# Embedding norm of a two-block transformer kernel: statistics from a second copy of x, rows normalised by VectorE alone

## The chip, the cores and the metric

The kernel runs on one core of a Trainium2 chip. The metric is the device time in microseconds (us) of one execution. TensorE (PE) multiplies matrices, VectorE (DVE) and ScalarE (ACT) work on tiles element by element, GpSimd (POOL) does so too and issues some transfers, and SyncE (SP) issues the others.

## The reference

Two blocks run one after the other on 512 tokens of width 2048. The change is in the very first step, the embedding norm `h = layernorm(x, emb_ln_g, emb_ln_b)`:

```python
def layernorm(x, g, b):
    xf = x.astype(jnp.float32)
    mu = jnp.mean(xf, axis=-1, keepdims=True)
    var = jnp.mean(jnp.square(xf - mu), axis=-1, keepdims=True)
    y = (xf - mu) * lax.rsqrt(var + LN_EPS) * g.astype(jnp.float32) + b.astype(jnp.float32)
    return y.astype(x.dtype)

def first_block(x, ...):
    h = layernorm(x, emb_ln_g, emb_ln_b)
    for l in range(DEPTH):            # DEPTH = 2
        h = hybrid_layer(h, ...)      # starts with proj = x @ w_in[l]
    return h
```

The layer rotates some columns by `cos(ang)` and `sin(ang)`, with `ang = positions * inv_freq`; these angles are the other thing the change moves.

## The kernel before, in words

All activations lie transposed in SBUF: 16 tiles `x_res` (`Y`) of 128 features by 512 tokens. A product in full precision is made of three passes of TensorE over one 128x512 tile (lines 331 to 333): `x_lo`·`w_hi`, `x_hi`·`w_lo`, `x_hi`·`w_hi`. So each activation tile is needed twice, as `x_hi` (ScalarE) and as the rest `x_lo` (VectorE, line 1109), and each weight unit of 128x1024 too: SP loads it into one of four slots, ScalarE copies it to `w_hi` (line 302), VectorE subtracts to get `w_lo` (line 325). The order on each engine is the order in which the code is written; semaphores join the engines.

**The start.** SP loads the positions, then x transposed in 16 tiles, then the first four weight units. VectorE turns the positions into angles (lines 989 to 1000), and ScalarE makes `cos_sin` from them. TensorE sums the first x tile over its features (`column_sums`), ScalarE makes of this a provisional mean `shift`, VectorE subtracts it from all 16 tiles (line 1194). Of each shifted tile ScalarE takes the squares (line 583), which TensorE adds up, and GpSimd adds the tiles themselves (line 420). `emb_end` (lines 1065 to 1074) turns the sums into a mean and a reciprocal of the deviation, both spread over all partitions. **The normalisation** then goes tile by tile: GpSimd subtracts the mean (line 390), VectorE multiplies by the reciprocal (line 1103), ScalarE writes `x_hi` and `x_res` with gain and offset (line 541), VectorE makes `x_lo` two tiles behind (line 1109).

**The first products** (`first_tiles`) work on three output tiles at once: nine passes for each of the feature tiles 0 to 7; then tiles 8 to 10 for each output tile alone, since the weight units 4 and 5 that two of them need are split only during the normalisation (`normalise(0, {13: ..., 14: ...})`); then nine passes for each of the feature tiles 11 to 15. That makes 144 passes. Output tile 3 follows with weight units 6 and 7, and in its middle (`lat_sums`, line 1881) it wants a sum from VectorE (line 1267), which stands on VectorE behind the split of unit 7. **GpSimd** waits for the last `x_lo`, issues four DMAs (lines 426, 428, 413) and scales all 16 `x_res` tiles without any wait between them (line 432).

The same normalisation is run again by two later layers (`normalise(1)`, `normalise_rms`), which keep their own way of taking statistics.

## Time and profile before

| | us |
|---|---|
| median of 3 runs | 2481.34 (2481.2 to 2482.8) |
| the profiled execution, whole | 2483.18 |
| its span in the trace | 2481.6 |
| TensorE busy | 2396.0 (97%) |
| VectorE busy | 1283.0 (52%) |
| ScalarE busy | 886.3 (36%) |
| GpSimd busy | 440.9 (18%) |

The profiled execution took 1.8 us more than the median, of which 1.6 us lie around its span. A row of a timeline gives start, duration, engine, line, what is written and read, and how often; a row of waits gives who waited for whom. `x12` in a row of a timeline stands for several instructions of one kind in a row, whose duration is that of them all.

### The profile page before, as it was taken

How to read it: one execution, taken by the hardware profiler on the slowest of the kernel's cores; microseconds unless marked ns; L12 is line 12 of the kernel's file. 1: busy time of each engine (PE TensorE's matmuls, PEld its weight loads, DVE VectorE, ACT ScalarE, POOL GpSimd, SP SyncE). 2: the span in 40 equal slices, each digit the busy share in tenths (PEclk: the TensorE clock that was granted, in tenths of full speed). 3: DMA queues.
4: the chain of work that ended last, by engine and by line, in shares of the span. 5: the costliest groups of instructions: out<-in, count | busy, mean ns of one | idle time of the engine just before them, and what ended most of it. 6: DMA issues, size and time to landing. Idle time of an engine off the chain costs nothing.

```text
span 2481.6 us, 31468 instructions
## 1 busy us (share of the span) xinstructions
PE 2396.0 (97%) x11426; PEld 1965.2 (79%) x11426; DVE 1283.0 (52%) x1823; ACT 886.3 (36%) x1340; POOL 440.9 (18%) x419
## 2 busy tenths in 40 slices
PE   4999999999999999999999999999999999999997
PEld 2888888888887788888788788788878888887886
DVE  8665543367645565543367765734255444444333
ACT  4522222366224422222266222522234544444221
POOL 6400000033402300000033301303001122222000
PEclk8999999999999999999999999999999999999998
DMA  3455554211322455553211223423322222223332
GB/s 142 146 182 177 170 181 140 85 52 60 102 94 76 157 178 170 184 178 130 83 56 62 87 91 112 144 87 102 100 85 74 79 76 76 76 76 113 116 101 76
DMA packets 78280, 277.68 MB, mean 112 GB/s; under 512 B 8832, under 2 KB 9088, under 8 KB 77824
## 3 DMA queue, kind: packets, MB, share of 16 engines
q1 hardware_dynamic: 61344, 213.29, 26.1%
q0 software_dynamic: 16864, 63.45, 7.4%
q8 instruction: 43, 0.70, 0.1%
q14 instruction: 29, 0.24, 0.0%
HBM read 268.31 MB, written 8.39 MB: 112 GB/s over the span
## 4 chain that ended last, share of the span: by engine, by line
PE 87%; DVE 6%; POOL 3%; issue 2%; ACT 2%; DVEq 0%; ACTq 0%; POOLq 0%
PE bank L331 27%; PE bank L333 27%; PE bank L332 27%; POOL sum L420 1%; DVE w_lo L325 1%; PE bank L2060 1%; DVE x_lo L1109 1%; POOL probs L407 1%; PE bank L1983 1%; POOL x_res L457 1%; ACT w_hi L302 0%; PE bank L2124 0%; PE bank L1823 0%; PE bank L1824 0%; DVE x_res L1722 0%
## 5 line engine op out<-in xcount | busy, mean ns | idle before, releaser
L333 PE MATMUL bank<-x_hi,w_hi 128*128 128x512 f32 x2880 | 1125.9, 391 | 0.0
L332 PE MATMUL bank<-x_hi,w_lo 128*128 128x512 f32 x2880 | 1124.7, 391 | 0.0
L331 PE MATMUL bank<-x_lo,w_hi 128*128 128x512 f32 x2368 | 946.3, 400 | 26.8 <-DVE x_lo L1109 17.5
L325 DVE SCALAR_TENSOR_TENSOR w_lo<-w_raw,w_hi 128x1024 fp32r<-128x1024 f32 (+1 forms) x384 | 488.3, 1275 | 754.8 <-ACT w_hi L302 754.4
L302 ACT ACTIVATE w_hi<-w_raw 128x1024 fp32r<-128x1024 f32 x390 | 407.5, 1048 | 938.1 <-PE bank L333 914.0
L333 PEld LDWEIGHTS bank<-x_hi,w_hi 128*128 128x128 f32 x2880 | 542.4, 188 | 115.2
L332 PEld LDWEIGHTS bank<-x_hi,w_lo 128*128 128x128 f32 x2880 | 543.7, 189 | 107.8 <-issue 2.2
L331 PEld LDWEIGHTS bank<-x_lo,w_hi 128*128 128x128 f32 x2368 | 447.1, 189 | 121.2 <-issue 24.4
L331 PE MATMUL bank<-mix_lo,w_hi 128*128 128x512 f32 x640 | 253.0, 395 | 7.3 <-DVE w_lo L325 6.1
L407 POOL TENSOR_SCALAR probs<-probs,stats 128x128 f32<-128x128 f32 (+3 forms) x128 | 138.6, 1089 | 671.8 <-DVE stats L1472 671.7
L413 POOL DMA_DIRECT2D ada_w<-wada x96 | 51.1, 533 | 551.2 <-DVE ada_w L969 551.2
L331 PEld LDWEIGHTS bank<-mix_lo,w_hi 128*128 128x128 f32 x640 | 121.2, 189 | 33.5 <-DVE w_lo L325 6.5
L779 ACT ACTIVATE probs<-bank,stats 128x128 f32<-128x128 f32 (+3 forms) x128 | 67.4, 528 | 142.1 <-DVE stats L1478 141.9
L969 DVE SCALAR_TENSOR_TENSOR ada_w<-ada_w,cond_b 128x1024 f32<-128x1024 f32 x96 | 114.2, 1219 | 0.9 <-DMA ada_w<-wada 0.9
L1478 DVE TENSOR_REDUCE stats<-bank 128x1 f32<-128x128 f32 (+3 forms) x128 | 60.9, 484 | 60.3 <-PE bank L2126 52.1
L517 ACT ACTIVATE squares<-x_res 128x512 f32 (+1 forms) x32 | 20.3, 633 | 170.5 <-DVE x_res L1420 153.3
L1420 DVE TENSOR_TENSOR x_res<-x_res,bank 128x512 f32 (+1 forms) x32 | 21.9, 686 | 85.3 <-PE bank L333 85.3
L489 POOL TENSOR_SCALAR k_gate<-gate_rows,ext_cols 64x512 fp32r<-64x512 f32 x16 | 28.5, 1784 | 157.7 <-issue 155.2
L457 POOL TENSOR_TENSOR x_res<-x_res,shift 128x512 f32<-128x512 f32 x28 | 48.6, 1769 | 27.6 <-ACT shift L521 27.6
L1463 DVE TENSOR_TENSOR pt_lo<-bank,pt_hi 128x128 fp32r<-128x128 f32 (+1 forms) x64 | 31.0, 486 | 39.6 <-ACT pt_hi L773 39.6
L333 PE MATMUL bank<-mix_hi,w_hi 128*128 128x512 f32 x128 | 50.4, 393 | 0.0
L332 PE MATMUL bank<-mix_hi,w_lo 128*128 128x512 f32 x128 | 50.1, 392 | 0.0
(330 smaller groups left out, 2273.9 us busy)
## 6 DMA issues: line engine op xcount, KB each, us to landing
w_raw<-stream SPq DMA_DIRECT2D x390, 512.0 KB, 3.5
ada_w<-wada POOLq DMA_DIRECT2D x96, 512.0 KB, 4.6
x_res<-xT SPq DMA_DIRECT2D x16, 256.0 KB, 5.6
x_res_spill<-x_res POOLq DMA_DIRECT2D x8, 512.0 KB, 6.1
x_res<-x_res_spill POOLq DMA_DIRECT2D x8, 512.0 KB, 6.3
outT<-x_res SPq DMA_DIRECT2D x16, 256.0 KB, 2.3
cond_b<-cond POOLq DMA_DIRECT2D x2, 1024.0 KB, 6.1
row_params<-rows POOLq DMA_DIRECT2D x1, 1536.0 KB, 8.6
```

Of the source, the lines that this page charges most:

```text
L302: nc.scalar.activation(WH[:, slot, :cols[n]], RAW[:, slot, :cols[n]], ACT.Copy).then_inc(w_hi, 1)
L325: nc.vector.scalar_tensor_tensor(out=WL[:, slot, :cols[n]], in0=RAW[:, slot, :cols[n]], scalar=1.0, in1=WH[:, slot, :cols[n]].bitcast(F32) ...
L331: nc.tensor.matmul(out, wh, xl, start=first, stop=False)
L332: nc.tensor.matmul(out, wl, xh, start=False, stop=False)
L333: return nc.tensor.matmul(out, wh, xh, start=False, stop=last)
L407: nc.gpsimd.tensor_scalar(pi, pi, ST[:, 12 + i:13 + i], None, ALU.mult).then_inc(S["p_norm"], 1)
L413: pool.dma_start(ADAB[:, n, :], wada[bass.ds(ADA_LAYER * l + n + 2 * i, 1), :, :] .rearrange("u p n -> p (u n)")).then_inc(S[f"ada_in{n}"] ...
L457: nc.gpsimd.tensor_tensor(out=Y[:, k, :], in0=Y[:, k, :], in1=SB[:, :], op=ALU.subtract)\
L779: nc.scalar.activation(PR[:, poff(i):poff(i + 1)], PS[banks[i]][:, :P * (i + 1)], ACT.Exp, bias=ST[:, 4 + i:5 + i], scale=scale, accum_out ...
L969: STT(out=ADAB[:, n % 2, :], in0=ADAB[:, n % 2, :], scalar=1.0, in1=CONDB[:, (n % 2) * UNIT:(n % 2 + 1) * UNIT], op0=ALU.mult, op1=ALU.mul ...
L1463: TT(out=PTL[i % 2][:, :P * (i + 1)], in0=PS[6 + i % 2][:, :P * (i + 1)], in1=PTH[i % 2][:, :P * (i + 1)].bitcast(F32), op=ALU.subtract).t ...
L1478: V.reduce_max(ST[:, 4 + i:5 + i], PS[banks[i]][:, :P * (i + 1)], axis=AXX, negate=True)\
```

## The change

x is loaded twice: first as `x_tokens`, four tiles of 128 tokens by 2048 features (1 MB each), then as before, transposed, behind the first three weight units. From `x_tokens` VectorE takes mean and variance of each token (16 `bn_stats` and 4 `bn_aggr`), ScalarE takes the root, and two diagonal matrices spread mean and reciprocal over all partitions by one matmul each (into PS[2] and PS[7]). The provisional mean, the squares, GpSimd's sums and `emb_end` are gone. In the normalisation of this first norm VectorE subtracts too, where GpSimd did. The second half of the angles stands behind the normalisation on VectorE, and their sine behind the third output tile on ScalarE. TensorE gets 8 and 20 small matmuls whose results nobody reads (`fill`).

```diff
@@ sync
+            for t in range(QB):
+                sp.dma_start(XN[:, t, :], xN[t]).then_inc(xn_in[t], 16)
+            for pos in range(SLOTS - 1):
+                load(0, pos)
+            sp.dma_start(EXT[:, :], extra).then_inc(S["cols_in"], 16)
+            sp.dma_start(COL[:, :], layers).then_inc(S["cols_in"], 16)
             for k in range(KT):
                 sp.dma_start(Y[:, k, :], xT[k]).then_inc(xt_in[k // 2], 16)
-                if k == 0:
-                    sp.dma_start(EXT[:, :], extra).then_inc(S["cols_in"], 16)
-                    sp.dma_start(COL[:, :], layers).then_inc(S["cols_in"], 16)
-            for pos in range(SLOTS):
-                load(0, pos)
+                if k == 4:
+                    load(0, SLOTS - 1)
@@ gpsimd
-            for k in range(1, KT):
-                pool.wait_ge(S["ct"], k + 1)
-                if k > 1:
-                    pool.wait_ge(S["emb_sum"], k - 1)
-                nc.gpsimd.tensor_tensor(out=A1[:, :], in0=Y[:, 0, :] if k == 1 else A1[:, :], in1=Y[:, k, :],
-                                        op=ALU.add).then_inc(S["emb_sum"], 1)
-            normalise_sub(0)
@@ scalar
-            act.wait_ge(S["ang"], 1)
-            nc.scalar.activation(CS[:, :], T0[:, :], ACT.Sin).then_inc(S["cs_done"], 1)
-            stat_shift(0)
-            for k in range(KT):
-                act.wait_ge(S["ct"], k + 1)
-                nc.scalar.activation(SQ2[:, k, :], Y[:, k, :], ACT.Square).then_inc(S["c_sq"], 1)
             for s in range(2):
-                split(0, s)
-            act.wait_ge(S["emb_v"], 4)
-            nc.scalar.activation(A2[:, :], A2[:, :], ACT.Sqrt).then_inc(S["emb_sd"], 1)
+                split(0, s, (0, 1) if s == 0 else (0,))
+                if s == 0:
+                    act.wait_ge(S["x_bn"], QB * (D // NT + 1) + 1)
+                    nc.scalar.activation(ST[:, 24:28], ST[:, 20:24], ACT.Sqrt).then_inc(S["x_sd"], 1)
             norm_end(0)
...
+                    if l == 0 and i == 2:
+                        act.wait_ge(S["ang"], 1)
+                        nc.scalar.activation(CS[:, :], POS[:, :], ACT.Sin)
@@ vector
+            def angles_end():
+                for part in (part1, part2, part3):
+                    rot(STT(out=posf[:, :], in0=turns[:, :], scalar=-part, in1=posf[:, :], op0=ALU.mult, op1=ALU.add))
+                rot(TS(posf[:, :], posf[:, :], ST[:, 2:3], PI_BELOW, ALU.add, ALU.min))
+                TS(posf[:, :], posf[:, :], -PI_BELOW, None, ALU.max).then_inc(S["ang"], 1)
+
+            def token_stats():
+
+                for t in range(QB):
+                    dve.wait_ge(xn_in[t], 16)
+                    for c in range(D // NT):
+                        V.bn_stats(BNX[:, t, c, :], XN[:, t, c * NT:(c + 1) * NT]).then_inc(S["x_bn"], 1)
+                dve.wait_ge(S["x_bn"], QB * D // NT)
+                for t in range(QB):
+                    V.bn_aggr(MVX[:, t, :], BNX[:, t, :, :]).then_inc(S["x_bn"], 1)
+                dve.wait_ge(S["x_bn"], QB * (D // NT + 1))
+                TS(ST[:, 20:24], MVX[:, :, 1], LN_EPS, None, ALU.add).then_inc(S["x_bn"], 1)
+                dve.wait_ge(S["pool_set"], 5)
+                for t in range(QB):
+                    TS(DG[0][:, t, :], IDN[:, :], MVX[:, t, 0:1], None, ALU.mult).then_inc(S["x_dg"], 1)
+                dve.wait_ge(S["x_sd"], 1)
+                V.reciprocal(ST[:, 28:32], ST[:, 24:28]).then_inc(S["x_ri"], 1)
+                dve.wait_ge(S["x_ri"], 1)
+                for t in range(QB):
+                    TS(DG[1][:, t, :], IDN[:, :], ST[:, 28 + t:29 + t], None, ALU.mult).then_inc(S["x_dg"], 1)
...
                 buf = NBUF[k % 4]
+                if n == 0:
+                    dve.wait_ge(xt_in[k // 2], 32)
+                    if k >= 4:
+                        dve.wait_ge(S["n_x"], norm_uses(0, k - 4))
+                    TT(out=buf[:, :], in0=Y[:, k, :], in1=PS[2][:, :], op=ALU.subtract).then_inc(S["n_sub"], 1)
...
-            emb_end()
-            normalise(0, {13: lambda: split(0, 2, (0,)), 14: lambda: split(0, 2, (1,))})
+            token_stats()
+            split(0, 0)
+            split(0, 1, (0,))
+            dve.wait_ge(S["x_bc"], 2)
+            normalise(0, {6: lambda: split(0, 1, (1,)), 13: lambda: split(0, 2, (0,)), 14: lambda: split(0, 2, (1,))})
+            angles_end()
@@ tensor
-            pe.wait_ge(xt_in[0], 32)
-            column_sums(0)
...
+            pe.wait_ge(xn_in[3], 16)
+            fill(8)
+            spread(S["x_dg"], QB, DG[0], 2).then_inc(S["x_bc"], 1)
+            spread(S["x_dg"], 2 * QB, DG[1], 7).then_inc(S["x_bc"], 1)
+            fill(20)
```

How the instructions stand, at two places. VectorE from the loads to the first `x_lo`, before (`tmp` are the angles, `sum` and `shift` the statistics and the mean):

```order
L998 SCALAR_TENSOR_TENSOR tmp_100<-tmp_102,tmp_100 128x512 x3
L999 TENSOR_SCALAR tmp_100<-tmp_100,stats 128x512
L1000 TENSOR_SCALAR tmp_100<-tmp_100 128x512
L1194 TENSOR_TENSOR x_res<-x_res,shift 128x512 x16
L325 SCALAR_TENSOR_TENSOR w_lo<-w_raw,w_hi 128x1024 x4
L1065 TENSOR_SCALAR shift<-bank 128x512
L1067 TENSOR_TENSOR sum_106<-shift 128x512
L1069 SCALAR_TENSOR_TENSOR sum_107<-bank,sum_106 128x512
L1072 TENSOR_SCALAR sum_107<-sum_107 128x512
L1074 RECIPROCAL bank<-sum_107 128x512
L1103 TENSOR_TENSOR centred<-centred,bank 128x512
```

and now (`bn_x` and `mean_var_x` are the statistics by token, `diag` the diagonal matrices):

```order
L1009 BN_STATS bn_x<-x_tokens 128x6 x16
L1012 BN_AGGR mean_var_x<-bn_x 128x2 x4
L1014 TENSOR_SCALAR stats<-mean_var_x 128x4
L1017 TENSOR_SCALAR diag_112<-ident,mean_var_x 128x128 x4
L1019 RECIPROCAL stats<-stats 128x4
L1022 TENSOR_SCALAR diag_113<-ident,stats 128x128 x4
L330 SCALAR_TENSOR_TENSOR w_lo<-w_raw,w_hi 128x1024 x3
L1113 TENSOR_TENSOR centred<-x_res,bank 128x512
L1115 TENSOR_TENSOR centred<-centred,bank 128x512
```

The long chain over 16 transposed tiles is replaced by one over four token tiles, and each tile's multiplication has a subtraction of VectorE's own ahead of it.

VectorE at the end of the normalisation, before: the last `x_lo`, then weight units 6 and 7, then the sum that TensorE wants in the middle of output tile 3:

```order
L1103 TENSOR_TENSOR sum_107<-sum_107,bank 128x512
L1109 SCALAR_TENSOR_TENSOR x_lo<-x_res,x_hi 128x512 x3
L325 SCALAR_TENSOR_TENSOR w_lo<-w_raw,w_hi 128x1024 x2
L1267 TENSOR_TENSOR tmp_100<-tmp_100,tmp_102 128x512
```

and now:

```order
L1115 TENSOR_TENSOR sum_111<-sum_111,bank 128x512
L1121 SCALAR_TENSOR_TENSOR x_lo<-x_res,x_hi 128x512 x3
L1000 SCALAR_TENSOR_TENSOR angles<-turns,angles 128x512 x3
L1001 TENSOR_SCALAR angles<-angles,stats 128x512
L1002 TENSOR_SCALAR angles<-angles 128x512
L330 SCALAR_TENSOR_TENSOR w_lo<-w_raw,w_hi 128x1024 x2
L1277 TENSOR_TENSOR tmp_104<-tmp_104,tmp_106 128x512
```

Five instructions of the angles moved from the start to between the last `x_lo` and the split of weight unit 6.

## Rows read from the trace of the kernel before

**Rows 1.** The page: busy time of TensorE, and the chain by line.

```profile
PE 2396.0 (97%) x11426; PEld 1965.2 (79%) x11426; DVE 1283.0 (52%) x1823; ACT 886.3 (36%) x1340; POOL 440.9 (18%) x419
```

**Rows 2.** TensorE's waits from 0 to 130 us: total, times, longest.

```profile
PE bank L331 <- DVE x_lo L1109: 15.6, 1, 15.6
...
PE bank L1881 <- DVE tmp L1267: 1.2, 1, 1.2
```

**Rows 3.** Timeline of the start: start, duration, engine, line, tiles, count, idle before.

```profile
6.76 2.15 DVE L998 SCALAR_TENSOR_TENSOR tmp<-tmp,tmp 128x512 f32<-128x512 f32 x3
...
9.46 0.43 DVE L1000 TENSOR_SCALAR tmp<-tmp 128x512 f32<-128x512 f32 x1
...
54.06 0.77 PE L331 MATMUL bank<-x_lo,w_hi 128*128 128x512 f32 x1 [15.60 <-DVE x_lo L1109]
```

**Rows 4.** Stretches: length, busy per engine, granted clock, DMA share, GB/s.

```profile
0.00:16.00 16.00, 5.57 (x7) 2.06 (x8) 10.23 (x31) 4.86 (x7) 4.47 (x12) 1.00 0.84 290
16.00:18.00 2.00, 2.00 (x6) 0.89 (x5) 2.00 (x3) 0.63 (x1) 1.86 (x2) 1.00 1.04 413
...
54.00:60.00 6.00, 5.93 (x14) 4.71 (x15) 6.00 (x8) 5.66 (x9) 6.00 (x4) 0.50 0.00 0
```

**Rows 5.** Timeline of VectorE elsewhere, where the kinds of added instructions run.

```profile
1665.37 4.85 DVE L1501 BATCH_NORM_STATS2 bn<-v_a 128x6 f32<-128x512 f32 x8
1670.25 0.43 DVE L1504 BATCH_NORM_AGGREGATE mean_var<-bn 128x2 f32<-128x12 f32 x4
...
787.47 0.88 DVE L1097 TENSOR_SCALAR diag<-ident,stats 128x128 f32<-128x128 f32 x4
...
836.95 2.35 DVE L325 SCALAR_TENSOR_TENSOR w_lo<-w_raw,w_hi 128x1024 fp32r<-128x1024 f32 x2
...
884.62 0.69 DVE L1281 COPY latents<-bank 64x512 f32<-64x512 f32 x1
885.35 0.69 DVE L1283 TENSOR_TENSOR bank<-bank,latents 64x512 f32<-64x512 f32 x1
```

**Rows 6.** Timeline of ScalarE around a table load.

```profile
102.73 0.60 ACT L611 ACTIVATE tmp<-bank 128x512 f32<-128x512 f32 x1 [2.50 <-PE bank L1888]
103.34 1.28 ACT L615 ACT_TABLE_LOAD   x1
104.64 1.92 ACT L615 ACTIVATE cond_b<-cond_b 128x2048 f32<-128x2048 f32 x1
```

**Rows 7.** Timeline of the normalisation: with GpSimd at work, then without.

```profile
69.75 1.18 DVE L1109 SCALAR_TENSOR_TENSOR x_lo<-x_res,x_hi 128x512 fp32r<-128x512 f32 x1
...
77.85 0.67 DVE L1103 TENSOR_TENSOR sum<-sum,bank 128x512 f32<-128x512 f32 x1
78.44 0.68 DVE L1109 SCALAR_TENSOR_TENSOR x_lo<-x_res,x_hi 128x512 fp32r<-128x512 f32 x1
...
81.53 0.69 DVE L1109 SCALAR_TENSOR_TENSOR x_lo<-x_res,x_hi 128x512 fp32r<-128x512 f32 x1 [0.60 <-ACT x_res L541]
```

**Rows 8.** Timeline behind the first norm: GpSimd's scaling, VectorE's unit 7, TensorE.

```profile
84.87 3.39 POOL L432 TENSOR_SCALAR x_res<-x_res,cols 128x512 f32<-128x512 f32 x5
...
91.28 4.79 DVE L325 SCALAR_TENSOR_TENSOR w_lo<-w_raw,w_hi 128x1024 fp32r<-128x1024 f32 x1 [7.58 <-ACT w_hi L302]
...
94.98 1.64 POOL L432 TENSOR_SCALAR x_res<-x_res,cols 128x512 f32<-128x512 f32 x1
...
97.21 0.94 PE L1881 MATMUL bank<-ones,tmp 128*128 128x1 f32 x7 [1.24 <-DVE tmp L1267]
```

**Rows 9.** The same place behind the second norm.

```profile
824.51 10.83 POOL L432 TENSOR_SCALAR x_res<-x_res,cols 128x512 f32<-128x512 f32 x16
...
831.02 5.40 DVE L325 SCALAR_TENSOR_TENSOR w_lo<-w_raw,w_hi 128x1024 fp32r<-128x1024 f32 x1 [7.55 <-ACT w_hi L302]
```

**Rows 10.** Stretches around another wait of TensorE (columns as in rows 4).

```profile
1396.00:1397.00 1.00, 0.94 (x2) 0.83 (x3) 1.00 (x2) 0.00 (x0) 1.00 (x1) 0.50 0.00 0
...
1401.00:1402.00 1.00, 1.00 (x5) 0.82 (x4) 1.00 (x3) 0.62 (x1) 0.00 (x0) 0.69 0.33 131
```

61 lines of the change are left out of this document (20 added, 41 removed).

## The prediction

> **What bounds the kernel now.** The page comes first: TensorE is busy 97% of the span [rows 1], so only its waits, its clock and its own work count. The list of its waits up to 130 us comes next: the longest by far is 15.6 us, until the first `x_lo` of the embedding norm [rows 2]. The timeline shows what it means: the first real product starts at 54.06 us [rows 3], and all that TensorE did ahead of it were sums for the statistics. From there it works on almost without a pause; the next wait is one of 1.2 us for VectorE's sum, in the middle of output tile 3, which ends at 97.21 us [rows 2, 8]. So everything behind 97.21 us should move by what the change moves this point, and I work out that point. 24 passes, half of output tile 3, lie ahead of the wait. Of the 144 + 24 passes up to there 14 fill the stretch from 54 to 60 us, at a granted clock of 0.50, that is 1.2 GHz [rows 4]; the other 154 end where the wait begins, at 97.21 - 1.24 = 95.97 us [rows 8], so one takes (95.97 - 60) / 154 = 0.23 us. Output tile 3 began at 95.97 - 24 x 0.23 = 90.5 us.
>
> **The new start.** Bytes set it first. SP's queue holds 0.26 MB of positions, 4.19 MB of tokens, 1.57 MB of weights, 0.14 MB of columns, then the transposed x. The queue moved 16 us x 290 GB/s = 4.64 MB in its first 16 us, and then 413 GB/s [rows 4]. The last token tile (4.46 MB in) thus ends at 15.6 us, weight unit 1 (5.50 MB) at 18.1 us, the first two x tiles (6.69 MB) at 21.0 us. I add 1 us for the signal to arrive, an estimate.
> VectorE has by then taken the statistics of the other token tiles. Eight `bn_stats` take 4.85 us [rows 5], so the last four end at 16.6 + 2.4 = 19.0 us; four `bn_aggr` 0.43, the epsilon about 0.2, the first diagonal 0.88 [rows 5]: 20.5 us.
> ScalarE copies unit 1 at 19.1 to 20.2 us, loads a table in 1.28 us [rows 6] and takes the root: 21.7 us. Here ScalarE is last. Then VectorE's reciprocal (0.3 with its gaps) and second diagonal (0.88) end at 23.0 us. Three `w_lo` at 2.35 / 2 = 1.17 [rows 5] end at 26.5 us. The spreading matmuls and the 20 fills lie beside them, and the x tiles have landed. So the normalisation starts at **26.5 us**.
> In the rows a table load starts 0.01 us behind the activation ahead of it, and the next activation 0.02 us behind the load [rows 6]. The Trainium skill, "ScalarE: Activation LUTs", section "What ACT_TABLE_LOAD costs", adds a drain of about 1380 ns to each switch; by it the start and the end would be 1.4 us later. The row shows no drain, so I go by the row.
>
> **The normalisation.** For each tile VectorE now subtracts, multiplies and makes `x_lo`. Instructions that depend on each other start 0.73 us apart (885.35 - 884.62 [rows 5]), others 0.59 us (78.44 - 77.85 [rows 7]): 0.73 + 0.60 + 0.60 = 1.93 us a tile. `x_lo` lasts 1.18 us while GpSimd works, 0.68 us when it is still [rows 7]. In the changed kernel GpSimd is still here, and I take the short one, 0.60 from start to start; the long one, 1.1, is the other end and gives 2.43 us a tile.
> The first `x_lo` starts behind three pairs, 26.5 + 3 x 1.33 = 30.5, and ends at 31.2; TensorE starts at **31.3** instead of 54.06 us. Its 144 passes take 6.0 us for the first 14 at half clock and 29.9 for the rest, and would end at 67.2 us if nothing were late. Late is weight unit 5, which stands on VectorE behind 14 pairs, 12 `x_lo` and three units: 26.5 + 18.6 + 7.2 + 3.5 = 55.8 us. Behind it TensorE has 54 passes, 12.4 us. So the first pass ends at **68.2 us** instead of 90.5: 22.3 us earlier.
> The last `x_lo` starts when ScalarE has written the last tile, about 60.7, and ends at 61.4 us (call it E). Before, the last `x_lo` ended at 81.53 + 0.69 = 82.22 us, and GpSimd began its scaling 2.65 us behind that [rows 7, 8]. Its four DMA issues lie between. So it begins at E + 2.6 = 64.0 us.
>
> **What is moved behind it.** The five instructions of the angles take 9.46 + 0.43 - 6.76 = 3.1 us [rows 3] and stand ahead of the split of weight unit 6. Before, unit 6 was split at once, ahead of GpSimd's scaling. Now VectorE comes to it at E + 3.0 = 64.4 us, 0.4 us behind GpSimd's start. This matters, because of two rows [rows 8, 9]: `w_lo` of unit 7 came while those 16 scalings ran, and took 4.79 and 5.40 us instead of 1.2. The scalings follow each other without a wait, 0.68 us apart. In one case VectorE got in ahead of the 16th (94.98 us, which then took 1.64 us), in the other it ended at 836.4, 1.07 us behind the end of the train at 835.34. In both it stood out five or six scalings. I read this as: once GpSimd's train runs, VectorE waits for its end.
> So unit 6, wanted at 68.2 us, is split when the train is over: it begins at 64.0, its 16th starts at 74.1 and it ends at 74.8, and `w_lo` ends 1.1 us later, at 75.2 to 75.9. I take 75.6. TensorE waits 7.4 us. In another wait of about 6 us the clock stood at 0.50 when it resumed at 1396 us, until about 1401.6 (0.69 in that slice) [rows 10]; 5.6 us at half cost 2.8 us. I add that. Unit 7 and the sum follow on VectorE by 78 us, ahead of need. TensorE comes to the sum at 75.6 + 5.5 + 2.8 = **83.9 us**, without its old wait, instead of 97.21: **13.3 us** saved.
> Hidden, by my reading: the later sine with two table loads instead of one (about 1.9 us of ScalarE, at a place where it idles before and after: 2.50 us before the row at 102.73 [rows 6]); the extra 4.19 MB (in the sum above); GpSimd's 37 us of removed work, which nothing else awaits. If ScalarE's 1.9 us are not covered they cost at most that.
>
> **Sum.** The profiled span would be 2481.6 - 13.3 = 2468.3; the execution shown lay 1.8 us over the median in all, so I put the difference on the median: 2481.34 - 13.3 = **2468.0 us**.
>
> **Rivals.**
> *Let in early* (0.17). VectorE reaches unit 6 ahead of GpSimd's first scaling, or slips in early; 0.4 us decide that. TensorE then does not stop for unit 6. Unit 7 is shut out instead, until 75.6, and the sum ends at 76.6 us: saved 20.5, **2460.8 us**. For it: the gap is small, and 1 of some 11 boundaries in rows 8 and 9 let VectorE in. Against: it is 0.4 us late by rows that repeat within 0.1.
> *One instruction at a time* (0.08). VectorE waits for the running scaling alone, 0.68 us. Unit 6 is split by 66.3, unit 7 by 71, the sum by 72.4, ahead of TensorE at 73.7: saved 23.5, **2457.8 us**. The 4.79 and 5.40 us speak against it. The Trainium skill says just this in "SBUF — State Buffer", section "SBUF: two separate sides": an exclusive lock, held for one instruction by whoever starts first. By that rule this would be the forecast; the rows disagree, since VectorE stood out five or six.
> *A slower tile* (0.11). `x_lo` keeps its 1.1 us, or the start slips by a late landing. With 12 x 0.5 = 6 us the whole of it moves: **2473.9 us**.
> *Slower than before* (0.03). TensorE, fed tile by tile, stays at 1.2 GHz through the whole first pass: 31.3 + 144 x 0.427 = 92.8 us, then 24 passes of which 14 are slow, 101.1 us, against 97.21: 3.9 later, **2485.2 us**, and more with a late start. It decides from some 53 us at half clock on. Against: at half clock a tile takes TensorE 3.8 us and VectorE 1.93, so it is never idle, and so fed the clock rose after 6 us [rows 4]. The Trainium skill, "TensorE: Matmul & The Clock Gate", "Part 1: The HAM clock gate", says that the idle array is throttled and activity releases it and under "HAM oscillation — how this bites in real kernels" shows a kernel that fell back at every tile; by the latter this rival would come about, 2485.2 us or more.
> The forecast has 0.60; 0.01 is left for the start gaining nothing at all.
>
> **How the numbers follow.** The forecast's own range is 2465 to 2471.5: start 1.5 us either way, clock 0 to 3 us, end of the train 0.7 us. The range of 2459 to 2474 takes in the early entry and the slower tile, and leaves out 0.08 + 0.04 and the tails. A measurement tells 0.2%, 5 us, from no change. All but the last rival and the remainder lie below 2476.4: faster 0.96; same 0.02 (the remainder, and a third of the slow rival, near its 2485.2); slower 0.02.
>
> **What would show it.** TensorE's first product at 31 us (30 to 33). `x_lo` at 0.68 us throughout. The end of unit 5's split near 56. GpSimd's scaling starting within 0.5 us of the end of the angles, and `w_lo` of unit 6, or the last angle instruction, lasting about 10 us. One wait of TensorE for `w_lo` of some 7 us near 68, followed by a clock of 0.50. Without that wait the first rival is right. If the first product is late, the bytes or ScalarE's root are; if TensorE waits between tiles, the tile's 1.93 us are wrong.

## The result

| | before | after |
|---|---|---|
| median of 4 runs each, us | 2482.07 | 2455.57 |
| lowest to highest | 2481.2 to 2483.7 | 2453.2 to 2456.1 |
| profiled span | 2481.6 | 2454.5 |

The ratio is 0.989, with a 95% interval of 0.9877 to 0.9902. The change saves 26.5 us. The prediction said 2468.0, with a range of 2459 to 2474: the direction was right, and the gain is nearly twice as large as forecast, outside the range.

The page of the kernel after, its line of busy times (against [rows 1]):

```profile
PE 2382.4 (97%) x11450; PEld 1965.4 (80%) x11450; DVE 1267.6 (52%) x1848; ACT 876.3 (36%) x1324; POOL 397.3 (16%) x388
```

TensorE's waits from 0 to 130 us, in total, times and longest (against [rows 2]):

```profile
PE bank L1747 <- DMA x_tokens<-xN: 14.9, 1, 14.9
PE bank L336 <- DVE x_lo L1121: 3.3, 2, 2.5
...
PE bank L336 <- DVE w_lo L330: 0.9, 2, 0.7
```

The wait of 15.6 us for `x_lo` and that of 1.2 us for the sum are gone. What is not there is what the forecast had put in: a wait of 7.4 us for `w_lo`.

Timeline of the start, from VectorE's reciprocal to the first product, and the start of the sum (L1889) in output tile 3 (against [rows 3] and [rows 8]; start, duration, engine, line):

```profile
20.00 0.18 DVE L1019 RECIPROCAL stats<-stats 128x4 f32<-128x4 f32 x1 [1.05 <-ACT stats L584]
...
21.00 3.49 DVE L330 SCALAR_TENSOR_TENSOR w_lo<-w_raw,w_hi 128x1024 fp32r<-128x1024 f32 x3
24.41 0.68 DVE L1113 TENSOR_TENSOR centred<-x_res,bank 128x512 f32<-128x512 f32 x1
...
28.37 0.68 DVE L1121 SCALAR_TENSOR_TENSOR x_lo<-x_res,x_hi 128x512 fp32r<-128x512 f32 x1
...
30.29 0.68 DVE L1121 SCALAR_TENSOR_TENSOR x_lo<-x_res,x_hi 128x512 fp32r<-128x512 f32 x1
...
52.48 1.22 DVE L330 SCALAR_TENSOR_TENSOR w_lo<-w_raw,w_hi 128x1024 fp32r<-128x1024 f32 x1
...
29.20 0.76 PE L336 MATMUL bank<-x_lo,w_hi 128*128 128x512 f32 x1 [2.47 <-DVE x_lo L1121]
...
71.56 0.95 PE L1889 MATMUL bank<-ones,tmp 128*128 128x1 f32 x8
```

The sum starts at 71.56 instead of 97.21 us, without a wait. That is 25.65 us, and the medians differ by 26.5: nearly the whole gain is made here, as the prediction's first step said. Only its size was wrong there, 13.3. The eight slow products in this trace are no part of that: in a second trace of the same kernel (after, again) there is none, and the sum starts at 71.39 us (see "The start").

The stretch behind the last `x_lo`, VectorE, then GpSimd (its four DMA issues end at 61.81):

```profile
58.52 0.69 DVE L1121 SCALAR_TENSOR_TENSOR x_lo<-x_res,x_hi 128x512 fp32r<-128x512 f32 x1 [0.39 <-ACT x_res L543]
59.13 2.14 DVE L1000 SCALAR_TENSOR_TENSOR angles<-turns,angles 128x512 f32<-128x512 f32 x3
61.30 0.80 DVE L1001 TENSOR_SCALAR angles<-angles,stats 128x512 f32<-128x512 f32 x1
62.14 0.81 DVE L1002 TENSOR_SCALAR angles<-angles 128x512 f32<-128x512 f32 x1
62.87 1.21 DVE L330 SCALAR_TENSOR_TENSOR w_lo<-w_raw,w_hi 128x1024 fp32r<-128x1024 f32 x1
67.02 1.30 DVE L330 SCALAR_TENSOR_TENSOR w_lo<-w_raw,w_hi 128x1024 fp32r<-128x1024 f32 x1 [2.95 <-ACT w_hi L307]
68.25 0.68 DVE L1277 TENSOR_TENSOR tmp<-tmp,tmp 128x512 f32<-128x512 f32 x1
...
61.84 3.38 POOL L432 TENSOR_SCALAR x_res<-x_res,cols 128x512 f32<-128x512 f32 x3
```

VectorE came to unit 6 (62.87) 1.0 us behind the start of GpSimd's train, where 0.4 had been forecast, and was not shut out. Neither was unit 7 at 67.02. It is mostly GpSimd that was held up: its first three scalings took 3.38 us instead of about 2.0; of VectorE's instructions the last one of the angles took 0.81 us, where it had 0.43 in [rows 3]. In the second layer the old picture of [rows 9] is still there, GpSimd's undisturbed train and a unit 7 that stands out five scalings:

```profile
798.86 11.74 POOL L432 TENSOR_SCALAR x_res<-x_res,cols 128x512 f32<-128x512 f32 x16
...
805.40 4.64 DVE L330 SCALAR_TENSOR_TENSOR w_lo<-w_raw,w_hi 128x1024 fp32r<-128x1024 f32 x1 [7.59 <-ACT w_hi L307]
```

So one kernel shows both. I call the door closed when VectorE is kept out of a running train of scalings until its 16th or its end, and open when VectorE gets in as soon as the running scaling is over. The question for the experiments is what closes it.

### The profile page after: what moved, and what is told of

It reads as the page before. It is cut to its first block, busy times and chain, and to the rows that moved or that the text cites. A ratio compares the mean times of both kernels' runs of the same rounds, so it can differ in the third digit from the quotient of the medians.

```text
span 2454.5 us, 31441 instructions
## 1 busy us (share of the span) xinstructions
PE 2382.4 (97%) x11450; PEld 1965.4 (80%) x11450; DVE 1267.6 (52%) x1848; ACT 876.3 (36%) x1324; POOL 397.3 (16%) x388
## 4 chain that ended last, share of the span: by engine, by line
PE 81%; issue 7%; DVE 6%; POOL 3%; ACT 2%; DMA 1%; SPq 0%; DVEq 0%; ACTq 0%; POOLq 0%
PE bank L336 25%; PE bank L338 25%; PE bank L337 25%; POOL x_res L457 2%; DVE w_lo L330 1%; DVE x_lo L1121 1%; PE bank L2068 1%; POOL probs L415 1%; PE bank L1991 1%; DMA w_raw<-stream 1%; ACT w_hi L307 0%; PE bank L2132 0%; PE bank L1831 0%; PE bank L1832 0%; DVE x_res L1732 0%
## 5 line engine op out<-in xcount | busy, mean ns | idle before, releaser
L457 POOL TENSOR_TENSOR x_res<-x_res,shift 128x512 f32<-128x512 f32 x28 | 48.5, 1769 | 27.7 <-ACT shift L521 27.7
```

The costliest lines, as they stand in the source:

```text
L457: nc.gpsimd.tensor_tensor(out=Y[:, k, :], in0=Y[:, k, :], in1=SB[:, :], op=ALU.subtract)\
```

## The experiments

All kernels are the changed one with the edit shown; the code is shortened. Since pauses late in the kernel move the end by some us either way (shown further down), the table gives, beside the time, how much earlier than in the kernel before one and the same copy of a weight unit on ScalarE starts at three places: in the first layer (141.15 us there), behind the second normalisation (871.70) and near the end (2412.40). These three columns are read from one execution of each kernel; the two of the changed kernel differ by 0.2 us in the first layer, and by 1.1 and 1.5 us at the later places. In brackets behind the time stands the number of runs; most kernels have one. The kernel before, measured beside them on four occasions, took 2481.9, 2482.6, 2483.7 and 2482.9 us.

| kernel | us (runs) | first layer | behind 2nd norm | near the end |
|---|---|---|---|---|
| after | 2455.57 (4) | 25.7 | 27.5 | 27.3 |
| after, again | 2456.57 (4) | 25.9 | 26.3 | 25.8 |
| early angles | 2464.29 (1) | 19.0 | 19.3 | 18.9 |
| late six | 2464.16 (1) | 14.7 | 15.1 | 18.4 |
| late six, gap | 2454.76 (1) | 24.7 | 28.1 | 27.8 |
| six in 2nd, 3rd | 2460.13 (1) | 15.8 | 18.0 | 22.4 |
| six in 3rd, 2nd | 2463.22 (1) | 15.8 | 18.8 | 19.3 |
| dummies in layer 2 | 2450.91 (1) | 25.8 | 28.7 | 31.6 |
| train of 24 | 2451.24 (1) | 25.7 | 28.6 | 31.3 |
| gap at the 9th | 2452.37 (1) | 25.3 | 27.5 | 30.1 |
| GpSimd waits | 2454.90 (1) | 25.7 | 28.8 | 28.4 |
| GpSimd subtracts | 2457.03 (1) | 25.9 | 26.7 | 26.3 |
| token tiles in pieces | 2459.34 (1) | 23.4 | 23.8 | 23.2 |
| no fills | 2451.98 (1) | 26.0 | 27.7 | 30.5 |
| start reordered | 2455.18 (4) | 27.1 | 26.4 | 25.9 |
| reordered, gap | 2449.67 (4) | 26.8 | 29.9 | 33.0 |
| all three | 2450.48 (4) | 26.4 | 29.2 | 32.1 |

### Is the lock-out real, and what does it cost?

**Early angles**: the five instructions stand ahead of the statistics.

```
-            angles_end()           # behind normalise(0, ...)
+            angles_end()
             token_stats()
```

> The angles are finished ahead of the token statistics, no longer behind the normalisation. The split of weight unit 6 then precedes GpSimd's train of 16 scalings, and only unit 7's split meets it. The five instructions take 3.1 us and push the statistics back by 2.2 us: normalisation start 26.6, first product 31.4 us, GpSimd's train from about 64.0 us, unit 7's split wanted at about 69.2 us, when seven or eight scalings have gone by undisturbed. Theory A (VectorE is shut out only by a train that has run undisturbed for some scalings; its own work at the head of the train kept it open in the changed kernel): unit 7's split takes 4.5 to 6.8 us instead of 1.30, the sum behind it is late by 2 to 4 us, and the kernel takes 2460 to 2462 us. Theory B (chance: each boundary between two scalings may or may not let VectorE in): 1.3 to 2 us in most cases, and 2457.5 us. Theory C (one instruction at a time): at most 1.9 us, 2457.5 us.

**Late six**: early angles, and a wait ahead of the split of unit 6.

```
             normalise(0, ...)
+            dve.wait_ge(S["res"], 4)
```

> As the kernel with the early angles, and the split of weight unit 6 waits in addition until four scalings of GpSimd's train have ended. This builds the situation of the prediction: VectorE comes to unit 6 when the train already runs, at about 66.8 us. Theory A and the prediction: it is shut out until the 16th scaling or the end, so the split ends at about 74.5 to 76 us; TensorE, which needs it at 68.3 us, waits 6 to 7.5 us and resumes at half clock for up to 5.6 us (0 to 2.8 us more); 2464 to 2468 us. Theory C: the split ends by 68.5 us, no wait of more than 0.5 us, 2458 us. Theory B lies between, with most weight near C.

**Late six, gap**: the same, and in GpSimd's train

```
                 for k in range(KT):
+                    if k == 2:
+                        pool.wait_ge(S["res"], KT * l + 2)
```

> As the kernel in which weight unit 6 waits for four scalings, where VectorE was shut out from the 5th scaling to the 16th (8.42 us for the split). The only difference: in each train the 3rd scaling waits until the 2nd has ended, so GpSimd runs dry once, for about 0.1 us, ahead of VectorE's request. Theory D (a train that has run from its start without a gap or an entry is closed, and one gap opens it for good): unit 6's split takes 1.2 to 2 us, unit 7's likewise, in both layers; TensorE's wait of 6.8 us goes: 2456 to 2458 us. Theory A in its first form (it is VectorE's own entry that opens the train, a gap far back does nothing): 8.4 us again, 2464 us.

Early angles, timeline: GpSimd's train, unit 7, and TensorE's wait at the sum:

```profile
62.62 11.74 POOL L432 TENSOR_SCALAR x_res<-x_res,cols 128x512 f32<-128x512 f32 x16
...
67.81 6.00 DVE L330 SCALAR_TENSOR_TENSOR w_lo<-w_raw,w_hi 128x1024 fp32r<-128x1024 f32 x1 [6.33 <-ACT w_hi L307]
...
74.96 1.47 PE L1889 MATMUL bank<-ones,tmp 128*128 128x1 f32 x8 [2.45 <-DVE tmp L1277]
```

Late six, the same place, with unit 6 and TensorE's first product behind its wait:

```profile
63.16 11.72 POOL L432 TENSOR_SCALAR x_res<-x_res,cols 128x512 f32<-128x512 f32 x16
...
65.91 8.42 DVE L330 SCALAR_TENSOR_TENSOR w_lo<-w_raw,w_hi 128x1024 fp32r<-128x1024 f32 x1 [5.37 <-POOL x_res L432]
...
74.38 0.79 PE L336 MATMUL bank<-x_lo,w_hi 128*128 128x512 f32 x1 [6.78 <-DVE w_lo L330]
```

Its stretches behind the wait (length, TensorE busy, granted clock, DMA share, GB/s):

```profile
74.00:76.00 2.00, 1.62 (x4) 0.50 0.25 45
76.00:80.00 4.00, 4.00 (x11) 0.50 0.88 274
```

Late six, gap, the same place, and unit 7 in its second layer:

```profile
65.24 1.71 DVE L330 SCALAR_TENSOR_TENSOR w_lo<-w_raw,w_hi 128x1024 fp32r<-128x1024 f32 x1 [5.50 <-POOL x_res L434]
67.59 1.66 DVE L330 SCALAR_TENSOR_TENSOR w_lo<-w_raw,w_hi 128x1024 fp32r<-128x1024 f32 x1 [0.64 <-ACT w_hi L307]
...
806.11 1.40 DVE L330 SCALAR_TENSOR_TENSOR w_lo<-w_raw,w_hi 128x1024 fp32r<-128x1024 f32 x1 [7.60 <-ACT w_hi L307]
```

What follows. The start is only 0.8 us later than in the kernel after (first product 29.96 us), less than the 2.2 expected. The whole kernel is slower than the 2460 to 2462 expected, 2464.29: behind the wait of 2.45 us the granted clock stood at 0.50 for 6.8 us, from 75.4 to 82.2, which costs another 3.4. Start, wait and clock are the 6.7 us that its first layer is behind. So in the changed kernel the later place of the angles was worth most by keeping the door open: where a gap holds it open (late six, gap) the first layer is only 1.0 us behind. Once unit 6 stands ahead of the train, the train runs undisturbed in the first layer too, and it is unit 7 that stands out from the 8th scaling to the 16th: 6.00 us, as theory A wanted. Late six builds the forecast's situation, and there its picture comes true nearly in its size: unit 6 from the 5th scaling to the 16th, a wait of 6.8 us (7.4 forecast), then a clock of 0.50 until 80 us. One wait of GpSimd on its own second scaling removes all of it: 8.42 us become 1.71, and the first layer ends 24.7 - 14.7 = 10.0 us earlier. The prediction had priced wait and clock at 7.4 + 2.8 = 10.2. **The price was right; the event did not take place.** Theory C (one instruction at a time) fails at a closed door and describes an open one: there VectorE waits for the running scaling alone. Theory B (chance at each boundary) doesn't fit either: trains of the same kind end the same way in every kernel, as the next section counts.

### What closes and opens the door?

**Dummies in layer 2**: five instructions of the angles' kind behind `normalise(1)`, on data that nobody uses.

```
                     normalise(l + 1, ...)
+                    for k in range(3):
+                        rot(STT(out=POS, in0=XL[0], scalar=1.0, in1=XL[1], ...))
+                    rot(TS(POS, POS, 0.5, 1.0, ...))
+                    rot(TS(POS, POS, 0.5, None, ...))
```

> The changed kernel, with five instructions of the angles' kind and size put behind the second layer's normalisation, ahead of the split of unit 6 there, so that VectorE is at work when GpSimd's second train begins. They compute nothing that is used. Theory A: the train is held up at its head as in the first layer (14 to 16 us instead of 11.74), and unit 7's split there takes 1.2 to 2 us instead of 4.64; TensorE's wait at the sum of the second layer (about 1.1 us) goes; the kernel is 0 to 1.5 us faster, 2454.5 us. Theory B: unit 7's split takes 4 to 5.5 us as before in the second layer, or by luck less. The prediction's reading (from its first scaling on a train shuts VectorE out to its end): one of the five, or unit 6's split, takes about 10 us.

**Train of 24**: eight scalings by one ahead of the sixteen, and a wait for them ahead of tile 8.

```
+                for k in range(8, KT):
+                    nc.gpsimd.tensor_scalar(Y_k, Y_k, 1.0, 0.0, mult, add).then_inc(S["extra"], 1)
                 for k in range(KT):
+                    if k == 8:
+                        pool.wait_ge(S["extra"], 8 * (l + 1))
```

> GpSimd's train is lengthened from 16 to 24 scalings in each layer by eight that multiply by one and stand ahead of the others. In the second layer VectorE comes to unit 7 with some ten scalings gone by, as before. If it is shut out until the end of the train, the split there takes 10 us (24 x 0.68 - 6.6) and TensorE waits 6 to 7 us for the sum, 2462 us. If it is shut out for a certain time or number of scalings, five or six, the split takes 4.6 us as now and the kernel stays at 2455.6 us within 1. In the first layer, where VectorE's work stands at the head of the train, theory A expects unit 7's split at 1.3 us again.

**Gap at the 9th**: as in late six, gap, with `k == 8` and `KT * l + 8`, on the changed kernel.

> The changed kernel with one wait in each train: the 9th scaling waits until the 8th has ended, so GpSimd's queue runs dry once, for about 0.1 us. VectorE comes to unit 7 of the second layer during the 10th, as before. The train of 24, in which VectorE was let in at once, had such a gap of 0.11 us behind its 8th. If the gap opens the door, the split takes 1.3 to 2 us instead of 4.64 and the sum is no longer late: about 1 us saved there. If the train of 24 let VectorE in for another reason (its length, or luck), the split takes 4.6 us as before. First layer: no difference, unit 7 at 1.3 us.

**Six in 2nd, 3rd** and **six in 3rd, 2nd**: early angles, and waits for `res` >= 1 in the first and >= 18 in the second layer, then >= 2 and >= 17.

> As the kernel with the early angles, and VectorE comes to weight unit 6 when one scaling of GpSimd's train has ended (first layer) and when two have ended (second layer). So far VectorE was let in at the next boundary where it asked during the first scaling of a train, and stood out to the 16th where it asked during the 5th or later with no entry before. Theory A (an entry early in the train keeps the door open, a train that starts alone shuts it): the border lies between the 1st and the 5th; if the first scaling alone shuts the door, both splits take 9 to 10 us and TensorE waits 6 us in both layers: 2470 us; if some scalings more are needed, both take 1.2 to 2 us: 2456 to 2459 us, and unit 7 behind them gets in at once as well. The prediction's reading (every request behind the start of the train stands out to its end): 9 to 10 us in both.

> As the kernel in which VectorE came to weight unit 6 when one scaling had ended in the first layer (shut out, 10.4 us) and when two had ended in the second (let in at once, 1.72 us), with the two numbers exchanged: two in the first layer, one in the second. If the number decides (a request in the 3rd scaling gets in, one in the 2nd doesn't), the first layer's split takes about 1.7 us and the second layer's 10.4. If the layer decides, it is 9.7 us in the first and 1.7 in the second. If neither rule holds (both shut out, or both let in), what closes the door stays open, and only the gap and VectorE's own earlier entry are shown to open it.

Dummies, second layer, VectorE:

```profile
798.58 0.81 DVE L1461 TENSOR_SCALAR angles<-angles 128x512 f32<-128x512 f32 x1
799.41 0.80 DVE L1462 TENSOR_SCALAR angles<-angles 128x512 f32<-128x512 f32 x1
800.25 1.59 DVE L330 SCALAR_TENSOR_TENSOR w_lo<-w_raw,w_hi 128x1024 fp32r<-128x1024 f32 x1
805.53 1.34 DVE L330 SCALAR_TENSOR_TENSOR w_lo<-w_raw,w_hi 128x1024 fp32r<-128x1024 f32 x1 [3.68 <-ACT w_hi L307]
```

Train of 24, second layer, GpSimd and unit 7; then unit 7 of gap at the 9th:

```profile
799.12 4.71 POOL L432 TENSOR_SCALAR x_res<-x_res 128x512 f32<-128x512 f32 x8
803.94 4.21 POOL L437 TENSOR_SCALAR x_res<-x_res,cols 128x512 f32<-128x512 f32 x4
...
805.58 1.48 DVE L330 SCALAR_TENSOR_TENSOR w_lo<-w_raw,w_hi 128x1024 fp32r<-128x1024 f32 x1 [7.55 <-ACT w_hi L307]
```

```profile
806.68 1.44 DVE L330 SCALAR_TENSOR_TENSOR w_lo<-w_raw,w_hi 128x1024 fp32r<-128x1024 f32 x1 [7.57 <-ACT w_hi L307]
```

Unit 6 in the first and the second layer, of six in 2nd, 3rd, and then of six in 3rd, 2nd:

```profile
63.61 10.44 DVE L330 SCALAR_TENSOR_TENSOR w_lo<-w_raw,w_hi 128x1024 fp32r<-128x1024 f32 x1 [3.36 <-POOL x_res L432]
...
811.09 1.72 DVE L330 SCALAR_TENSOR_TENSOR w_lo<-w_raw,w_hi 128x1024 fp32r<-128x1024 f32 x1 [3.94 <-POOL x_res L432]
```

```profile
63.83 9.76 DVE L330 SCALAR_TENSOR_TENSOR w_lo<-w_raw,w_hi 128x1024 fp32r<-128x1024 f32 x1 [4.04 <-POOL x_res L432]
...
809.60 1.73 DVE L330 SCALAR_TENSOR_TENSOR w_lo<-w_raw,w_hi 128x1024 fp32r<-128x1024 f32 x1 [3.27 <-POOL x_res L432]
```

Two things open the door, by edits that change little else. VectorE at work while the train starts: with five dummies unit 7 of the second layer takes 1.34 instead of 4.64 us. And one gap in the train, 0.11 us long in the train of 24 (803.83 to 803.94): unit 7 takes 1.48 and 1.44 us with ten and nine scalings gone by, and 1.43 us in the second layer of reordered, gap, where the gap stands ahead of the 3rd. The dummies are seen in one execution, the gap in one execution each of four kernels. Once open it stayed open: in late six, gap, unit 7 of the second layer came eight scalings behind the gap and took 1.40 us. The train of 24 thus answered another question than it was made for; since it held the gap, whether a longer train would shut VectorE out longer wasn't tried.

My rule "a train that starts alone shuts the door" is not the whole of it. It held in twelve cases: both layers of the kernel before [rows 8, 9], of early angles and of late six, and the second layer of the kernel after, in both its profiles, and of the four kernels below that change only the start or the subtraction (4.64 to 4.72 us each). But a request in the 2nd or 3rd scaling was shut out in the first layer, both times, and let in in the second, both times. VectorE came equally late in both layers, 0.7 us behind the start of the train for the 2nd scaling and 1.4 us for the 3rd. The exchange of the numbers shows that the layer decides there and not the number. What differs between the layers for that is **still open**.

### Taking the contention away, and the other half of the change

**GpSimd waits**: both trains start only when VectorE's first sum is done.

```
+                pool.wait_ge(S["sq_sum"], 4 * l + 1)
                 for k in range(KT):
```

> The changed kernel, with both trains of GpSimd held back until VectorE has finished the first sum of the latents, so that nothing of them lies beside the splits of units 6 and 7. First layer: the angles' last two instructions return to 0.49 and 0.43 us, units 6 and 7 to 1.2; the sum was not waited for, so 0 to 0.5 us are saved. Second layer: unit 7 takes 1.2 instead of 4.64 us and TensorE's wait of about 1.1 us at the sum goes. The train then lies beside the diagonals and the later splits and may shut VectorE out there; if it does, a wait of 2 to 6 us appears at the next weight or at the latents' broadcast, and this kernel is slower than the changed one. Without that: 2454 us.

Nothing is gained in the first layer (25.7 in both). In the second, TensorE's wait of 1.1 us at the sum is gone, and the kernel stands at 28.8 against 27.5 us. The second trace of the changed kernel stands at 26.3 there: the wait was 1.2 us long in it, and the clock fell behind it (0.72 on average from 812 to 818 us, where the first trace has 1.00). So in the changed kernel the contention costs 1.1 to 1.2 us of waiting and, in one of two traces, half clock on top; none of it in the first layer.

**GpSimd subtracts**: the part "VectorE alone" is undone.

```
+            act: wait x_bc >= 1; SB = Copy(PS[2])
+            pool: for k in range(KT): NBUF[k % 4] = Y[k] - SB
-            dve:  TT(out=buf, in0=Y[:, k, :], in1=PS[2], op=subtract)
```

> One part of the change undone: GpSimd subtracts the mean again in the first normalisation (ScalarE copies the mean out of the bank for it), and VectorE only multiplies and makes x_lo. By the rows of before a tile then takes VectorE 0.60 + 1.10 = 1.70 us, since x_lo lasts 1.18 us beside GpSimd; in the changed kernel it is 1.92. TensorE works 2.0 us on a tile, so it is VectorE's lead that decides. The prediction's view: the last x_lo ends 16 x 0.22 = 3.5 us earlier, the two waits of TensorE for x_lo (3.3 us) and the two for w_lo (0.9) shrink, 0 to 4 us saved: 2452 to 2455.6 us. Rival: GpSimd's instructions shut VectorE out in this stretch too, or the first x_lo is late by the copy of the mean, and it is 1 to 5 us slower.

Its first product and two tiles on VectorE:

```profile
30.44 0.77 PE L336 MATMUL bank<-x_lo,w_hi 128*128 128x512 f32 x1 [3.29 <-DVE x_lo L1128]
...
29.15 1.14 DVE L1128 SCALAR_TENSOR_TENSOR x_lo<-x_res,x_hi 128x512 fp32r<-128x512 f32 x1
...
30.81 1.17 DVE L1128 SCALAR_TENSOR_TENSOR x_lo<-x_res,x_hi 128x512 fp32r<-128x512 f32 x1
```

A tile takes 30.81 - 29.15 = 1.66 to 1.70 us instead of 1.92, and the first product is 1.2 us later, behind the copy of the mean. The two cancel: the first layer stands at 25.9 against 25.7 and 25.9 us. Both the hope and the rival were right in half. That VectorE alone normalises is worth nothing in time. What is left of the change for its gain is the earlier mean and variance, with the angles out of VectorE's way and the door open.

### The start

**Token tiles in pieces**: each tile in four loads of 512 columns.

```
+                for c in range(0, D, NT):
+                    sp.dma_start(XN[:, t, c:c + NT], xN[t][:, c:c + NT])
```

> Each token tile is loaded in four pieces of 512 columns (2 KB a row instead of 8 KB), the same bytes. In the changed kernel the last tile landed at 14.95 us; the prediction had 16.6 us, from the 290 GB/s that the kernel before reached in its first 16 us with tiles of 2 KB a row, where the changed kernel reached 332. If the length of the rows sets that rate, the last tile lands near 16.6 us again and everything behind it comes 1.6 us later: 2457.2 us. If the rate has another cause (what else the queue carried), it lands at 15.0 us and the time stays at 2455.6; if it is the issue of the many DMAs on SP's queue, it lands later than 16.6 us and the weight units move too.

Two stretches of its start, then the same two of the kernel after (length, TensorE busy, clock, DMA share, GB/s):

```profile
2.00:9.00 7.00, 0.00 (x0) 1.00 0.81 255
12.00:15.00 3.00, 0.00 (x0) 1.00 1.05 405
```

```profile
2.00:9.00 7.00, 0.00 (x0) 1.00 0.96 335
12.00:15.00 3.00, 0.05 (x1) 1.00 1.00 418
```

Over the first 16 us the rate is 283 GB/s, like the 290 of the kernel before [rows 4], against 332 in the kernel after. The last tile lands at 17.2 instead of 14.95 us, and the first layer is 2.3 us later. So how the tokens are cut into transfers is what made the forecast of the bytes wrong. Whether it is the length of the rows stays open, since the edit also makes 16 transfers of four. SP issues them until 10.60 us instead of 3.84, the DMA share is only 0.81 from 2 to 9 us (0.96 in the kernel after), and from 12 to 15 us the same rows of 2 KB move at 405 GB/s. The tile lands later than 16.6 us and the weight units are 2.2 us later (ScalarE's first copy at 18.35 instead of 16.11), which is what the third reading, that of the issues, expected. The second reading fails.

**No fills**: both `fill` calls of the start are left out (their results are unused).

> The changed kernel without the 28 filling matmuls of TensorE around the two spreads of mean and scale (their results are used by nobody). They keep TensorE at work until 26.7 us, 2.5 us ahead of the first product, and the clock then stood at 0.50 for about eight products, until 32.6 us, against 14 products in the kernel before. If the fills are what brought the clock up early, without them the first 14 products or more run at half clock, 6 x 0.2 = 1.3 us or more later, up to 3 us: 2457 to 2458.5 us. If they do nothing, 2455.6 us.

**Start reordered**: ScalarE copies unit 0, takes the root, then copies unit 1; VectorE splits unit 0 ahead of the reciprocal.

```
-                split(0, s, (0, 1) if s == 0 else (0,))          # act
+                split(0, s, (0,))                                # act
                 ... Sqrt ...
+                    split(0, 0, (1,))                            # act
+                split(0, 0, (0,))                                # dve
                 dve.wait_ge(S["x_sd"], 1)
```

> The start of the changed kernel in another order: ScalarE copies one weight unit instead of two ahead of its root, and VectorE splits that unit while the root is taken, where it stood idle for about 1 us. In the changed kernel the second copy ended at 18.45, the table load at 19.75 and the root at 19.97 us; now the load can begin at 17.2, the root stands at 18.5 to 19.0 us. VectorE: first diagonal to 18.9, the split to 20.0, reciprocal and second diagonal to 21.1, two splits to 23.4 us. The normalisation starts at 23.4 instead of 24.41 and the first product 1 us earlier. The prediction's view of the start (a chain of bytes, statistics, root, diagonals and splits, with TensorE following tile by tile) expects 1.0 us of it to stay: 2454.5 us. Rival: TensorE is then held up later in the pass, since the x tiles or weight unit 5 don't come earlier; 2455.6 us.

First products of the kernel without fills, of the reordered one, and of the changed kernel run again, unchanged:

```profile
28.94 0.77 PE L336 MATMUL bank<-x_lo,w_hi 128*128 128x512 f32 x1 [5.98 <-DVE x_lo L1121]
```

```profile
27.80 0.47 PE L336 MATMUL bank<-x_lo,w_hi 128*128 128x512 f32 x1 [1.33 <-DVE x_lo L1123]
```

```profile
29.00 0.47 PE L336 MATMUL bank<-x_lo,w_hi 128*128 128x512 f32 x1 [2.46 <-DVE x_lo L1121]
```

Without fills the first layer stands at 26.0 against 25.7 and 25.9 us: in the changed kernel the fills give nothing to the time. The slow products are no measure of them. Eight products run slowly (0.63 us each instead of 0.39) in the first trace of the changed kernel, seven in the kernel without fills, and none in the changed kernel run again, behind the same pause of 2.46 us. They cost next to nothing: with eight such products the sum in tile 3 starts at 71.56 us, with none at 71.39. VectorE sets the pace there: without slow products TensorE waits longer for `x_lo`, 4.3 us in all instead of 3.3. In the reordered kernel the pause is 1.33 us long, and no product is slow either. Its first layer ends 1.4 us earlier, a little more than the 1.0 expected. But the whole kernel gained nothing, 2455.18 against 2455.57 us. The next section says where that went.

## Where the late differences come from

Two pauses of TensorE stand in each layer's attention, 3.0 and 1.5 to 1.6 us long, for `qn_lo` and `x_lo`, the same in the kernel before and in those compared here. Stretches of TensorE around them (length, busy, clock, DMA share, GB/s), of the kernel after and then of the reordered one:

```profile
460.00:480.00 20.00, 15.05 (x72) 0.91 0.10 39
```

```profile
460.00:480.00 20.00, 15.07 (x69) 0.87 0.08 27
```

And a later one, of the kernel after and then of that with the dummies:

```profile
1195.00:1230.00 35.00, 30.42 (x144) 0.90 0.12 42
```

```profile
1195.00:1230.00 35.00, 30.41 (x160) 0.95 0.14 46
```

TensorE's busy time agrees to 0.02 us and its waits to 0.1; only the granted clock differs. The reordered kernel loses 1.9 us at the first place (27.1 to 25.2). The one with the dummies gains 1.2 us near 1225 us, 0.5 near 1380, 1.9 near 1540 and 1.1 near 1840, gives 1.7 back by 2272, and the kernel after gets nothing of this. From 900 to 2430 us the clock record has 34.1 us at 0.50 in the kernel after, in its second trace, in the reordered kernel and in GpSimd waits, and 27.3 us in the one with the dummies, in reordered, gap and in all three. The difference of 6.8 us at half speed is worth 3.4 us. So a kernel's time holds up to some 4 us that hang on how long the clock stays at 1.2 GHz behind pauses that no edit touched. What decides it I can't say: two kernels that stand at the same point ahead of these pauses fall on different sides (GpSimd waits goes from 28.8 to 28.4, the one with the dummies from 28.7 to 31.6). That is why single edits were judged by the columns of the table and not by the end.

**After, again**:

> The changed kernel once more, unchanged, in five rounds, beside the two improved kernels of this call: 2455.6 us, with single runs between 2453 and 2456.5, and the same waits of TensorE in its first 130 us. If the pauses behind the second layer bring the clock back sooner in some of its runs, single runs near 2451 us appear too.

It stayed between 2455.3 and 2456.8 us; no run came near 2451.

**Reordered, gap** joins the reordered start and the gap ahead of the 3rd scaling:

> The reordered start (first product 1.3 us earlier, gain at the end of the first layer's input tiles 27.1 against 25.7 us) and one gap in each train of GpSimd, ahead of its 3rd scaling, which let VectorE in at once in both layers. Second layer: unit 7's split 1.4 instead of 4.64 us, TensorE's wait of 1.1 us at the sum gone. By the two places the kernel should gain 1.3 + 1.1 = 2.4 us on the changed one, 2453.2 us; the clock in later pauses adds or takes up to 2 us either way and may hide it.

**All three** joins the reordered start, the held back trains, and

```
                     if k >= 2:
-                        lo(k - 2)
+                        lo(k - 2)      # for n == 0: lo(0) stands behind tile 1, lo(1) behind tile 3
```

> The reordered start, the trains held back until VectorE's first sum is done (which let nothing be shut out in either layer), and x_lo of the first tile made behind two tiles' pairs instead of three. The first product comes 1.3 us earlier by the first edit and 0.9 more by the last (27.0 us); TensorE is then fed at VectorE's pace of 1.92 us a tile while it works at half clock, so both should stay. Expected: 1.3 + 0.9 + 1.2 = 3.4 us under the changed kernel, 2452.2 us. Rival: the x_lo of later tiles or weight unit 5 is then late by the same 0.9 us and it ends at 2453.1 us.

The first of them is the best kernel of this study: 2449.67 us (2449.5 to 2450.0), a ratio of 0.9867 to the kernel before (0.9851 to 0.9883), and 6.9 us less than the changed one measured beside it. By the table it is 0.9 to 1.1 us ahead in the first layer, 2.4 to 3.6 behind the second norm, and 5.7 to 7.2 near the end; the last 3.3 to 3.6 us come behind pauses that no edit touched, and are the clock's (the 3.4 us above). All three gets its first product at 27.04 us, 0.8 ahead of the reordered kernel's 27.80, but reaches the sum in tile 3 at 70.72 instead of 70.18 us. Its rival was right in kind: VectorE's pace, not the first product, then sets the end of the pass.

## Why the prediction was wrong, by its steps

- **What bounds the kernel, and that the sum of tile 3 is the point to work out**: right. 25.65 us were saved there, 27.1 at the end of the profiled span.
- **The new start**: 26.5 forecast, 24.41 us measured. 1.65 of the 2.1 us are the bytes: the last token tile landed at 14.95 instead of 16.6, and ScalarE's copy of weight unit 1, which the root stands behind, began at 17.39 instead of 19.1. The term that was mis-sized is the 290 GB/s from [rows 4], a rate of 16 tiles of 256 KB in rows of 2 KB, used for four tiles of 1 MB in rows of 8 KB, which came at 332; the kernel with the pieces shows that this cut of the transfers matters, not which part of it. The rest is in the steps behind it: the root stood at 19.97 (forecast 21.7), the second diagonal at 21.1 (23.0). By the Trainium skill, "ScalarE: Activation LUTs", section "What ACT_TABLE_LOAD costs", it should have been 1.4 us later still. The load began 0.02 us behind the copy, and the root 0.01 us behind the load: no drain, as the row had said.
- **The normalisation**: a tile takes 1.92 us (1.93 forecast), the first product comes 4.8 us behind the start (4.8), unit 5 is split 29.3 us behind it (29.3). Half clock lasted for eight products in one trace and for none in the other, not for 14, and the two reach the sum 0.2 us apart. GpSimd's being still makes `x_lo` short, as assumed.
- **The path without the shut-out**: from first product to sum the prediction had 73.7 - 31.3 = 42.4 us; it took 71.56 - 29.20 = 42.4. That the clock was wrong did not matter, since unit 5 on VectorE set the end of the pass in the sum too.
- **What is moved behind it**: this step failed. "Once GpSimd's train runs, VectorE waits for its end" was read from two cases in which VectorE came from an idle stretch of 7.6 us into the 10th scaling of a train that had run alone. In the changed kernel VectorE was at work when the train began (61.30 and 62.14 against 61.84 us), and that is one of the two things that keep the door open in the runs: the dummies open it so in the second layer, and the early angles, which take it away, find it closed in the first. The 10.2 us of wait and clock fall away. With the 2.1 of the start and rounding they are the whole difference, 25.65 - 13.3 = 12.35 us.
- **The rivals**: "One instruction at a time", with 0.08, named this outcome and 2457.8 us, 2.2 from the result. With the true start it would have been 2455.7. The Trainium skill says the same in "SBUF — State Buffer", section "SBUF: two separate sides". The kernel after agrees with it in the first layer, and the 4.64 us in its second layer and the 10.44 us of six in 2nd, 3rd do not: a lock of one instruction is not what those traces show. "Let in early" gave unit 6 the right fate for the wrong reason, and had unit 7 shut out: by early angles, that is what happens if VectorE is early by being done. "Slower than before" did not come: eight slow products, then full speed.
- **The range**: its low end, 2459, took the start as sure to 1.5 us inside one case and put only 0.08 on the open door. Three or four rows of a stall from a single situation are a price, not a law of when it occurs. The two bounds of the unknown, shut out or let in, lay 10 us apart, and the range should have held both.

## What to carry to other kernels

When a stall in the trace is used for another place, check that the waiting engine arrives in the same way: idle or at work, into the same kind of queue. If a trace has the stall only in one situation, the range takes in its absence. A long train of GpSimd instructions without a wait can shut VectorE out for its whole length; one wait inside it, on its own earlier instruction, costs 0.1 us and removed a wait of 6.8 us and 10.0 us of the first layer here. And before something small in one trace is given a cause, a second trace of the same kernel shows whether it is there again: the slow first products were not.

## What the runs showed of the hardware

- GpSimd's trains of 16 scalings, 0.67 us apart, let VectorE in only ahead of the 16th or at the end in 14 cases (4.6 to 10.4 us for an instruction of 1.2), and at once in two (1.72 and 1.73 us, second layer of six in 2nd, 3rd and of six in 3rd, 2nd). One gap of 0.1 us earlier in the train was enough in every case with such a gap.
- At an open door it is GpSimd that loses: one scaling beside VectorE takes 1.6 to 2.8 us instead of 0.69, and in the kernel after the train lasts 15.6 instead of 11.7 us.
- The same 4.19 MB land 2.2 us later in 16 transfers with rows of 2 KB than in four with rows of 8 KB (283 against 332 GB/s in the first 16 us). Rows of 2 KB alone don't set that rate: from 12 to 15 us they moved at 405 GB/s.
- TensorE's clock behind one and the same pause can differ: behind 2.46 to 2.47 us eight of the first products of the changed kernel were slow in one trace and none in the other. In the kernel without fills the granted clock reads 1.00 over the slow products (11 matmuls in 4.1 us, columns as above), so there the duration of a product is the better witness:

```profile
28.90:33.00 4.10, 4.06 (x11) 1.00 1.04 403
```
